# Second block of a fused two-block kernel: the two exponentials of an attention pair one slot later on ScalarE, and one reciprocal for both rows

## The reference

```python
# forgetting attention ("fox"): per head, per block of 128 queries
s = einsum(q_block, k[:, :e]) * sm_scale + F[q] - F[k]      # F = cumsum(log f), causal mask
p = softmax(s); out = p @ v
# sparse attention ("dsa"): the same with a mask of the 128 keys that an indexer's score picks
score = sum_h iw[h] * relu(iq[h] . ik); sel = top_k(score, 128)
s = where(selected, q . k * sm_scale, -inf); p = softmax(s); out = p @ v
# around them
z = rmsnorm(x) @ w_in_2          # 31 column units of 128: q, k, v, gates, pooling, indexer
mixed = concat(pool * silu(.), dsa * silu(.), fox * silu(.));  out = rmsnorm(x + mixed @ w_out_2)
```

## Time and profile before

| | us |
|---|---|
| median of 3 runs (1310.92 to 1311.26) | 1310.95 |
| the profiled execution | 1310.9 |
| its span | 1309.2 |
| TensorE busy | 1288.6 (98%) |
| VectorE busy | 828.8 (63%) |
| ScalarE busy | 575.3 (44%) |
| GpSimd busy | 249.1 (19%) |

### The profile page before, as it was taken

The page is one execution under the profiler, slowest core; times in us unless marked ns, Lnnn a source line. Parts: engine busy times, 40 slices in busy tenths (PEclk is TensorE's granted clock), DMA queues, the critical chain, the costliest instruction groups (busy, mean ns, idle before and its releaser), DMA issues.

```text
span 1309.2 us, 20297 instructions
## 1 busy us (share of the span) xinstructions
PE 1288.6 (98%) x6833; PEld 1028.6 (79%) x6833; DVE 828.8 (63%) x1715; ACT 575.3 (44%) x997; POOL 249.1 (19%) x484
## 2 busy tenths in 40 slices
PE   8999999999999999999999999999999999999998
PEld 6777878878788788888788888888877766767686
DVE  6976666676676753444477763477766688885723
ACT  5654535445454432223344432244454455555422
POOL 2513304033140300001200000000023023366300
PEclk9999999999999999999999999999999999999999
DMA  6323232232232223333233323333234322222221
GB/s 184 90 66 89 80 88 79 73 88 79 74 88 77 71 83 92 96 96 106 79 106 96 92 82 97 114 96 96 66 91 117 91 89 81 80 66 65 65 65 65
DMA packets 210051, 114.43 MB, mean 87 GB/s; under 512 B 7696, under 2 KB 206671, under 8 KB 210005
## 3 DMA queue, kind: packets, MB, share of 16 engines
q1 hardware_dynamic: 210005, 113.84, 30.0%
HBM read 111.70 MB, written 2.13 MB: 87 GB/s over the span
## 4 chain that ended last, share of the span: by engine, by line
PE 89%; DVE 7%; issue 2%; ACT 1%; DMA 0%; SPq 0%; DVEq 0%; POOLq 0%; ACTq 0%; POOL 0%
PE gb L671 75%; PE gb L1150 2%; PE gd L1150 1%; PE gd L1101 1%; PE gd L1078 1%; PE gd L1091 1%; DVE wlo L1624 1%; DVE selb L2191 1%; PE gd L779 1%; PE gd L871 1%; PE gd L862 1%; PE gd L767 0%; PE gd L850 0%; PE gd L851 0%; DVE selb L2202 0%
## 5 line engine op out<-in xcount | busy, mean ns | idle before, releaser
L671 PE MATMUL gb<-act_a,whi 128*128 128x512 f32 x2656 | 898.2, 400 | 2.5 <-DVE wlo L1624 2.5
L671 PEld LDWEIGHTS gb<-act_a,whi 128*128 128x128 f32 x2656 | 498.9, 188 | 121.3 <-issue 17.0
L671 PE MATMUL gb<-act_a,wlo 128*128 128x512 f32 x1416 | 552.3, 390 | 0.0
L1624 DVE TENSOR_TENSOR wlo<-raw,whi 128x1024 fp32r<-128x1024 f32 x189 | 236.0, 1249 | 149.1 <-ACT whi L1182 148.3
L1182 ACT ACTIVATE whi<-raw 128x1024 fp32r<-128x1024 f32 x211 | 223.2, 1058 | 216.9 <-PE gb L671 186.4
L671 PEld LDWEIGHTS gb<-act_a,wlo 128*128 128x128 f32 x1416 | 266.6, 188 | 48.3 <-issue 1.0
L671 PE MATMUL gb<-act_b,whi 128*128 128x512 f32 x432 | 152.5, 393 | 0.1
L671 PEld LDWEIGHTS gb<-act_b,whi 128*128 128x128 f32 x432 | 81.1, 188 | 17.4 <-DVE qc L1901 0.5
L2439 POOL TENSOR_TENSOR zs<-zs,ca 128x512 f32<-128x512 f32 x3 | 5.5, 1838 | 322.1 <-ACT ca L1185 322.1
L2471 POOL TENSOR_TENSOR wlo<-raw,whi 128x1024 fp32r<-128x1024 f32 x22 | 53.1, 2413 | 57.4 <-ACT whi L1182 57.4
L671 PE MATMUL gb<-act_b,wlo 128*128 128x512 f32 x128 | 49.9, 390 | 0.0
(11 more groups left out here) (467 smaller groups left out, 1558.9 us busy)
## 6 DMA issues: line engine op xcount, KB each, us to landing
raw<-in_w_in_dram SPq DMA_DIRECT2D x102, 512.0 KB, 3.4
raw<-in_w_up_dram SPq DMA_DIRECT2D x44, 512.0 KB, 3.6
raw<-in_w_down_dram SPq DMA_DIRECT2D x16, 384.0 KB, 3.1
raw<-in_w_down_dram SPq DMA_DIRECT2D x16, 320.0 KB, 3.1
raw<-in_w_a_out_dram SPq DMA_DIRECT2D x8, 512.0 KB, 3.4
raw<-in_w_b_out_dram SPq DMA_DIRECT2D x8, 512.0 KB, 3.4
raw<-in_w_o_dram SPq DMA_DIRECT2D x8, 512.0 KB, 3.4
raw<-in_w_out_dram SPq DMA_DIRECT2D x8, 512.0 KB, 3.5
```

The source lines that it names most:

```text
L671: ins = pe.matmul(gb[:, b, :], l, r, start=(first and m == 0), stop=(last and m == len(todo) - 1))
L1624: dve.tensor_tensor(wlo[:, i % 2, 0:k * P], raw[:, i % 4, 0:k * P], whi[:, i % 2, 0:k * P].bitcast(F32), ALU.subtract).then_inc(split_read ...
```

## The change

The exponentials leave the step "s" on ScalarE. A new step "exp" of the same row stands one slot later, with priority 1, behind the "t" step (priority 0) of the same slot. The other engines don't know "exp" and keep their "s". On VectorE the even row's "weigh" waits for both exponentials of its pair and takes the reciprocal of two columns; the odd row's has none.

```diff
@@ schedule()
                 todo.setdefault(start + 4 * n + 3 + t % 2, []).append((5, ("weigh", c, t)))
                 todo.setdefault(start + 4 * n + 5 + t % 2, []).append((0, ("t", c, t)))
                 todo.setdefault(start + 4 * n, []).append((3, ("s", c, t)))
+                todo.setdefault(start + 4 * n + 1, []).append((1, ("exp", c, t)))
@@ ScalarE, beside(e)
-                elif what == "s":
+                elif what == "exp":
                     _, c, t = e
                     n = pair_step(c, t)
                     sc.wait_ge(max_ready, n + 1)
@@ VectorE, beside(e), "weigh"
                     k = n % 4
-                    dve.wait_ge(exp_ready, n + 1)
-                    link(dve.reciprocal(small[:, 24 + k:25 + k], small[:, 12 + k:13 + k]))
+                    if t % 2 == 0:
+                        dve.wait_ge(exp_ready, n + 2)
+                        link(dve.reciprocal(small[:, 24 + k:26 + k], small[:, 12 + k:14 + k]))
                     p = prob[k][:, 0:(c + 1) * P]
                     dve.tensor_scalar(p, p, small[:, 24 + k:25 + k], None, ALU.mult).then_inc(p_ready, 1)
```

## The result

The changed kernel takes 1316.45 us (median of 6 runs, 1315.32 to 1316.97), against 1311.2 for the kernel before on the same chip: a ratio of 1.0038, 95% interval 1.0029 to 1.0048. It is slower by 0.4%, and above the predicted range. Its profiled execution took 1315.64 us, with a span of 1313.9, 4.7 more than before. The difference is read in that span first. Lines of the changed kernel are numbered one or two higher: L1064 is L1065, L1091 is L1092, L2228 is L2230.

What follows compares the result with a forecast made beforehand. TensorE was taken to bound the kernel, holding 89% of the chain, with 6.0 us of waits to win. The terms +1.4 - 0.95 + 0.8 + 1.7 + 0.2 - 0.6 - 0.6 - 0.95 gave +1.0: 1311.9 us, range 1309.7 to 1314.2.

Steps and rivals of the forecast that it cites:

- Reciprocals: On VectorE, 48 become 24: 3.8 us less busy, no losing wait resting on it, hidden elsewhere beside TensorE's work.
- Group 0, first pair: Exponentials behind Silu and two table loads make TensorE 3.15 us late, 1.75 absorbed by later waits: cost +1.4 us.
- forecast 1069.11: Time at which the unit's matmuls in group 0 were to go on, instead of 1065.96.
- Unit 11: Wait at 1094.06: weight rounding goes ahead of the exponentials, so the copy comes earlier; gain 0.95 us.
- turn_v of groups 1 to 4: Odd copies behind table load and exponentials make TensorE wait: +0.8 and +1.7 us, then +0.1 each.
- 1169.27: Wait in group 3: the copy goes first, VectorE's weighing comes next, 0.2 earlier; gain 0.6 us.
- 1228.89 and 1237.70: Two waits in group 5: the copy no longer runs behind late exponentials; gains 0.6 and 0.95 us.
- sign of being wrong: New waits before "t" steps, released by VectorE, in the changed profile; no size given.
- Losses only: Rival: GpSimd's shifted subtractions meet VectorE's work and replace the waits won, losses stay; +4.1, 1315.0 us, chance 0.09.
- That gains and losses add: VectorE and ScalarE wait again for TensorE's products after each place, so the terms were summed; +1.0 us.

Runs made afterwards that it cites:

- recip_only: The kernel before with only the two-column reciprocal per pair, exponentials in their old slot; 1311.21 us, ratio 0.9999.
- exp_only: The changed kernel with one reciprocal per row again, so the exponentials' move alone; 1318.88 us, ratio 1.0053.
- fill: The changed kernel with twelve unread 128x512 matmuls on TensorE in front of the product that waits in group 0; 1314.23 us.
- pair2_own: The changed kernel with the exponentials of the second pair of groups 1 and 2 in their old slot; 1313.6 us.
- mixed_late: The changed kernel with exponentials in their old slot for group 0's first pair and the second pair of groups 0 to 4; 1309.22 us, ratio 0.9985.
- hold_v: four_late with GpSimd's subtractions held: unit 22's until a group 3 weighing is over, unit 29's until group 5's values are written; 1310.33 us.
- four_late: The changed kernel with exponentials late in only four of 24 pairs, those costed as gains; 1309.34 us, ratio 0.9985.

## Why the prediction was wrong

The sign of the sum was right, and so was the mechanism of seven of its eight terms; its size was not. Two effects stood in no term and make the miss: TensorE's clock behind the stall of group 0, and GpSimd holding VectorE in groups 3 and 5. By its own steps:

- **Reciprocals**: right in the sum (recip_only, 0.0), with 0.160 us for two columns against the 0.16 taken. That "none of the losing waits rests on it" holds too. The 3.8 us that VectorE was to save don't show: it is as busy in recip_only as before, and 8.5 us busier in the changed kernel. That they are worth nothing elsewhere is wrong by accident: without the shorter path the gain of unit 11 is a loss (exp_only), 1.4 us.
- **Group 0, first pair, +1.4**: the term that was mis-sized. Product and unit went on at 1068.10 and 1069.61, just at the 0.5 us of that run behind the forecast 1069.11, and fill shows 1.3. The step that failed is the silent one that a stall costs its own length. Behind 3 us of standing still TensorE ran at half clock for 3.4 us (1.6 us) or 6.8 (2.6 to 3.1). In the middle the trace before has no such stretch, and neither has any kernel here without such a stall; but its last 2 us, behind TensorE's last matmul, were a sign that the clock falls when TensorE stands still, and a bound should have been asked for.
- **Unit 11, -0.95**: right, -0.98, with 0.34 us left of the wait.
- **turn_v of groups 1 to 4, +0.8, +1.7, +0.1 and +0.1**: right, within 0.1 us each (pair2_own takes the first two away). The price of the table load from its row was right: 1.28 us, and the exponential starts 0.01 later, at 1067.27. The Trainium skill ("ScalarE: Activation LUTs", What ACT_TABLE_LOAD costs) adds a drain of 1380 ns; the trace doesn't agree.
- **1169.27, -0.6**: wrong, +0.2, and +0.3 behind it. The step that failed is the length of "VectorE's weighing" that "comes next, 0.2 earlier". It did come 0.2 earlier, at 1173.02, but it took 1.42 us and not the 0.55 of the earlier trace rows, since GpSimd's scaling started with it; the 0.87 us between them make up the miss of 0.8. In the third pair the weighing qc, held by the subtraction, makes the +0.3. The sum had no term for one engine holding another, and a wait in front of a "t" step that VectorE ends is what the prediction itself named as a sign of being wrong.
- **1228.89 and 1237.70, -0.6 and -0.95**: right, -0.71 and -0.95, but 0.83 came back between them at turn_v of group 5, a place that the prediction didn't look at: there a weighing of 1.46 us, held by the subtraction, makes VectorE write the values late.
- **The rivals**: *Losses only* named the mechanism that decided groups 3 and 5, GpSimd meeting the weighings, and put it at the right place (though at 1174.50 it is the scaling and not the subtraction); but two gains and unit 11's stayed, so that it didn't come true in its own form. Its 1315.0 lay nearest to what happened. The case that I left out is the clock. The rest of the way from 4.7 in the profiled execution to 5.2 in the medians is in the runs with the longer half clock: those at 0.996 to 0.997 take 0.7 to 1.4 us more span than the profiled one at 0.998.
- **That gains and losses add** was right to 0.1 us where the same instructions met: unit 11 gave 0.95 to 0.98 us in every kernel but exp_only that has its pair late, and turn_v of group 1 took 0.84 to 0.87. It was not where the meetings changed: unit 11 lost 0.46 in exp_only, and the second pair of group 3 lost 0.2 in the changed kernel and gained 0.5 in mixed_late.

## What to carry to other kernels

Price a new stall on TensorE at its length plus the half clock that may follow it: here a wait of 2.9 us cost 1.6 to 3.1 us more than itself. An instruction that makes TensorE wait 3 us in one piece should stay where it was; waits of 0.7 and 1.6 us cost only themselves. Before VectorE's or GpSimd's instructions are moved by some tenths of a microsecond, list which of them come to lie side by side: a 0.3 us instruction that starts with a 2.4 us one of GpSimd takes 2.5. And test a change of order pair by pair: here 4 of 24 pairs gained as much as 18 (1308.8 us with one hold on GpSimd), and three others held most of the loss.

## What the hardware showed

- A stall of 2.9 us by its row goes with a half clock in all six profiled executions that have it: for 3.4 us, beginning 2.2 or 2.3 us after TensorE had gone on, or for 6.8 us, beginning between 0.5 us before and 0.9 us after. Filled with twelve matmuls it doesn't, nor do stalls of 0.68 and 1.59 us, nor one of 2.0 (hold_v).
- VectorE's TENSOR_SCALAR, its COPY and its operations on two SBUF tiles stand still until GpSimd's subtraction ends: 2.48 us for 128x128, 2.25 for a copy of 128x8, 2.25 for 64x16. It works both ways: the subtraction of 2.40 took 2.92 when one of VectorE was in front of it. Beside the same subtraction VectorE's gate, with one input from PSUM, took its 0.68 us (at 1093.93 in the changed kernel). The Trainium skill ("SBUF — State Buffer", SBUF: two separate sides) calls the pair of ports that the two engines share an exclusive lock, held for the whole instruction, whose loser fully blocks: the traces agree. It gives the lock to whichever starts first: by the recorded starts that doesn't hold at 0.05 us and less, since the weighings at 1095.72 (exp_only), 1170.38 (four_late) and 1176.40 start 0.02, 0.03 and 0.05 us ahead of the subtraction and are held.
